# Gate and up products of experts 1 to 15 with the weights as the stationary operand, in halves of 64 array columns, and the turned token rows streamed

## The reference

```python
def ec_moe(x, router_w, w_gate, w_up, w_down):
    ...
    cap = n_tok * EC_CAPACITY // N_EXPERTS          # 64 sample tokens, 16 prompt tokens
    aff = jax.nn.softmax(jnp.einsum('btd,de->bte', x, router_w).astype(jnp.float32), axis=-1)
    gate, idx = lax.top_k(jnp.swapaxes(aff, 1, 2), cap)
    xe = x[bidx, idx]
    hid = jax.nn.silu(jnp.einsum('becd,edf->becf', xe, w_gate)) * jnp.einsum('becd,edf->becf', xe, w_up)
    ye = jnp.einsum('becf,efd->becd', hid, w_down) * gate[..., None].astype(x.dtype)
    return jnp.zeros_like(x).at[bidx, idx].add(ye)
```

## Time and profile before

| | |
|---|---|
| runs, us | 1419.07, 1413.60, 1416.11 (median 1416.11) |
| profiled execution: first to last instruction | 1413.9 us |
| PE busy | 1331.0 us (94%) |
| PE weight loads busy | 815.3 us (58%) |
| DVE, ACT, POOL busy | 697.4, 528.6, 280.4 us |
| mean granted TensorE clock | 0.982 of full |
| DMA | 333.82 MB, of which SP's queue 310.11 MB |

### The profile page before, as it was taken

The page is one execution under the profiler, slowest core; times in us unless marked ns, Lnnn a source line. Parts: engine busy times, 40 slices in busy tenths (PEclk is TensorE's granted clock), DMA queues, the critical chain, the costliest instruction groups (busy, mean ns, idle before and its releaser), DMA issues. The chain is left out here.

```text
span 1413.9 us, 27268 instructions
## 1 busy us (share of the span) xinstructions
PE 1331.0 (94%) x11153; PEld 815.3 (58%) x11153; DVE 697.4 (49%) x1634; ACT 528.6 (37%) x1221; POOL 280.4 (20%) x239
## 2 busy tenths in 40 slices
PE   5999998889899999999998999989899999999996
PEld 1755666766686444444448999555588444444443
DVE  1536614677635343334346646956654433334436
ACT  2723113666423222222226468665532322222213
POOL 0001103586002011111110030655301101111101
PEclk8999999999999999999998999999999999999997
DMA  9688961041526999999982012050043999999995
GB/s 364 237 328 304 350 217 27 23 158 34 194 107 257 369 377 375 374 378 373 387 307 74 1 64 68 1 223 1 1 183 125 374 368 378 378 377 381 376 350 180
DMA packets 105800, 333.82 MB, mean 236 GB/s; under 512 B 23182, under 2 KB 29164, under 8 KB 99532
## 3 DMA queue, kind: packets, MB, share of 16 engines
q1 hardware_dynamic: 99276, 310.11, 57.9%
q0 software_dynamic: 5824, 19.86, 5.9%
q10 hardware_dynamic: 576, 2.10, 0.4%
HBM read 308.13 MB, written 23.89 MB: 235 GB/s over the span
## 5 line engine op out<-in xcount | busy, mean ns | idle before, releaser
L1961 PE MATMUL psum<-wraw,proj 128*32 128x512 f32 x3072 | 399.6, 594 | 2.7 <-ACT proj L2071 1.2
L1967 PE MATMUL psum<-wraw,proj 128*16 128x256 f32 x3072 | 234.1, 379 | 0.6 <-ACT proj L2076 0.6
L1967 PEld LDWEIGHTS psum<-wraw,proj 128*16 128x16 f32 x3072 | 89.8, 97 | 229.5 <-issue 224.6
L1961 PEld LDWEIGHTS psum<-wraw,proj 128*32 128x32 f32 x3072 | 96.2, 110 | 74.1 <-issue 8.5
L1927 POOL DMA_INDIRECT x_rows<-modrow,idx x30 | 42.8, 1427 | 452.7 <-DVE modrow L2176 452.7
L2089 ACT ACTIVATE proj<-psum 128x320 f32<-128x320 f32 x32 | 14.0, 437 | 286.0 <-PE psum L2027 286.0
L2138 DVE TENSOR_SCALAR proj<-psum,proj 128x64 f32<-128x64 f32 x232 | 55.7, 313 | 106.5 <-PE psum L1949 106.5
L1336 POOL TENSOR_SCALAR ring<-ring,small 128x640 f32<-128x640 f32 x48 | 90.2, 1883 | 40.6 <-DVE small L1275 40.1
L2171 DVE SCALAR_TENSOR_TENSOR modrow<-psum,proj 64x512 f32<-64x512 f32 x60 | 44.9, 749 | 84.3 <-PE psum L1967 83.9
L2163 DVE TENSOR_TENSOR proj<-proj,psum 64x512 f32<-64x512 f32 x32 | 22.1, 690 | 128.1 <-ACT proj L2096 128.1
L1266 DVE TENSOR_REDUCE small<-psum 128x1 f32<-128x640 f32 (+1 forms) x80 | 57.3, 717 | 53.2 <-PE psum L1241 52.8
(11 more groups left out here) (520 smaller groups left out, 2437.6 us busy)
## 6 DMA issues: line engine op xcount, KB each, us to landing
wraw<-in_exp_w_gate_dram SPq DMA_DIRECT2D x128, 512.0 KB
wraw<-in_exp_w_up_dram SPq DMA_DIRECT2D x128, 512.0 KB
wraw<-in_exp_w_down_dram SPq DMA_DIRECT2D x128, 512.0 KB
ring<-in_ada_w_dram SPq DMA_DIRECT2D x29, 1024.0 KB, 6.5
hold<-in_ada_w_dram SPq DMA_DIRECT2D x14, 1024.0 KB, 6.6
ring<-in_ev_w_in_dram SPq DMA_DIRECT2D x4, 2048.0 KB, 12.3
xr<-x_rows SPq DMA_DIRECT2D x15, 512.0 KB, 7.4
proj<-in_ada_w_dram SPq DMA_DIRECT2D x5, 1024.0 KB, 9.0
```

The lines of the kernel that those rows point to most:

```text
L1961: mm = pe.matmul(psum[quad(q, 32), b, :], xs[:, quad(q % 2, 32)], pair[q // 2], start=first, stop=last)
L1967: mm = pe.matmul(psum[quad(q, CAPP), b, 0:QP], xs[:, CAPS:CAP], pair[q // 2][:, q % 2 * QP:(q % 2 + 1) * QP], start=first, stop=last)
```

## The change

The gate and up products of experts 1 to 15 swap their operands. The stationary operand is now 64 columns of weights; two such halves stand beside each other in the array's columns, and through each the 80 token columns of `xgT` (sample and prompt tokens together) are streamed. For each of the 8 blocks k, each of the two matrices and each of 4 blocks f of 128 hidden positions there are two matmuls of 64 x 80: 128 matmuls an expert where there were 64. The result has hidden positions in partitions and tokens in columns, in one bank for gate and one for up, which is what the down product needs: `turn_hidden` and `turned_hidden` are left only for expert 0. ACT has one silu of 128 x 320 and DVE one product of 128 x 320 straight into `hidT`, of which there are now two, for even and odd experts. Hidden position f x 128 + p now stands in partition p of block f, so the down matrices are loaded row by row in that order (`load_weights`, n == 2): each of the four DMAs reads one unbroken 512 KB, as 128 pieces of 4 KB as before. PSUM banks are dealt out anew: 5 and 3 for odd, 2 and 6 for even experts' hidden rows, 4 and 7 for down, and `tensor_last` goes to bank 0.

```diff
         def load_weights(sp, l, m, ready):
             n, e = EXPERT_ORDER[m]
-            src = A[EXPERT_W[n]][l, e].rearrange("(p k) n -> p (k n)", p=P)
...
+            if n == 2:
+                src = A[EXPERT_W[n]][l, e].rearrange("(f p) n -> f p n", p=P)
+                pieces = [src[i] for i in range(PARTS)]
+            else:
+                src = A[EXPERT_W[n]][l, e].rearrange("(p k) n -> p (k n)", p=P)
+                pieces = [src[:, i * w:(i + 1) * w] for i in range(PARTS)]
...
                 def into_hidden(e, h):
...
                         if e >= 2:
-                            pe.wait_ge(s["hid"], e)
+                            pe.wait_ge(s["hid"], e - 1)
...
                     for k in range(4 * h, 4 * h + 4):
-                        pair = [wraw[m % NSLOT][:, k * 512:(k + 1) * 512] for m in (gate_at, up_at)]
-                        samples(5, xgT[:, e % 2, k, :], pair, k == 0, k == KD - 1)
-                        mm = prompts(3, xgT[:, e % 2, k, :], pair, k == 0, k == KD - 1)
+                        rows = xgT[:, e % 2, k, :]
+                        for m, b in zip(both, hidden_banks(e)):
+                            for f in range(FB):
+                                for c in range(0, P, WT):
+                                    at = k * 512 + f * P + c
+                                    mm = pe.matmul(psum[c:c + WT, b, f * CAP:(f + 1) * CAP], wraw[m % NSLOT][:, at:at + WT], rows,
+                                                   start=(k == 0 and f == 0), stop=(k == KD - 1), skip_group_check=True)
...
                 for e in range(1, NE):
                     into_hidden(e, 0)
-                    turn_hidden(e - 1)
-                    if 1 < e < NE - 1:
+                    if e == 1:
+                        turn_first_hidden()
+                    elif e < NE - 1:
                         turn(e + 1)
...
                     down(e - 1)
-                turn_hidden(NE - 1)
                 if following:
                     following["tensor_last"](pe)
                 down(NE - 1)
...
                 def gate_hidden(e):                                   # ACT
                     act.wait_ge(s["mm"], PLACE_OF[1, e] + 1)
...
+                    act.activation(sgT, bank(hidden_banks(e)[0], FB * CAP), ACT.Silu).then_inc(s["hs"], 1)
...
                 def hidden(e):                                        # DVE
...
+                        dve.wait_ge(s["mm"], PLACE_OF[2, e - 2] + 1)
+                    dve.wait_ge(s["hs"], 3 + e)
+                    dve.tensor_tensor(hidT[e % 2], sgT.rearrange("p (f c) -> p f c", c=CAP), bank(hidden_banks(e)[1], FB * CAP).rearrange("p (f c) -> p f c", c=CAP),
+                                      ALU.mult).then_inc(s["hid"], 1)
```

86 lines of the change are left out of this document (46 added, 40 removed).

## The result

The kernel after takes 1424.10 us (median of 11 runs, 1419.23 to 1428.51), the kernel before 1416.29 us (11 runs on the same chip): ratio 1.0055, 95% interval 1.0039 to 1.0072. That is 7.8 us slower, where 1410 and a gain of 6 had been forecast. The profiled execution took 1424.36 us with a span of 1421.7 us.

What follows compares the result with a forecast made beforehand. The prediction took the weight DMAs (18.9 us an expert against PE's 17.1) as the bound; 1413.9 - 2.4 (layer 0) - 3.5 (layer 1) = 1408.0 us of span, plus 2.2 gave 1410 us, range 1400 to 1430.

Steps and rivals of the forecast that it cites:

- PE's new time: Experts on PE: gate and up products take 9.0 us, the period 15.5 us an expert, 1.6 less than before.
- Were PE alone the bound, 2 x 15 x 1.6 = 48 us would go: Both layers' expert stages: 48 us would be saved if only PE set the pace.
- Rival A: Gate and up products: PE cannot be fed, a pair costs over 0.19 us, total 1512 or 1560 us; chance 0.12.
- The pace of the weights: Expert weight loads: DMAs need 6.29 us a matrix, 18.9 us an expert, and keep that pace.
- What makes PE faster turns almost wholly into waiting for weights: Expert stages: PE catches the DMAs up near expert 9, then waits some 3 us an expert.
- the DMAs are slower than PE: Expert stages before the change: DMAs slower by 1.8 us an expert, living on ten slots filled ahead.
- Its start can move forward by about 0.3 us; I take 0.5: Start of expert 15: up 15 lands at 710.0, PE starts at 710.26, so only 0.5 us is gained.
- rival B: Instruction fetches: 0.48 MB more cost 29 us on one DMA engine, 2 us if spread; 1415 to 1439, chance 0.08.
- C: Clock rival: idling halves PE's clock; catching expert 15 in both layers loses up to 3.5 us each; 1412 to 1418, chance 0.10.
- I take 3.5: End of layer 1: terms sum to 3.6 us, rows read back only some 2.5 us earlier, so 3.5 us gained.
- the 1.35 us between the two down products: Between down 14 and down 15: with the turning of hidden rows gone, layer 1 saves all 1.35 us.
- 0.34 for faster: Chance of a time under 1409.0 us: 0.4 of the forecast's 0.60 plus rival D's 0.10.

Runs made afterwards that it cites:

- light traffic: Kernels before and after, loading only the first ten expert matrices of each layer, later products reading what stands in the slots: 1416.56 us (before) and 1369.05 us (after).
- split prompts: Kernel before with each 256-column prompt-row matmul of experts 1 to 15 split into two of 128: 1422.89 us, ratio 1.0045.
- only 15 in halves: Kernel before with the new products for expert 15 alone, in both layers, and the new layout of down throughout: 1419.88 us, ratio 1.0021.
- padded_before: Kernel before with 240 more wait instructions per expert on TensorE's queue in experts 1 to 15: 1731.55 us, ratio 1.2221.
- pool_padded: Kernel before with 240 more wait instructions per expert on GpSimd's queue in experts 1 to 13, both layers: 1581.55 us, ratio 1.1168.
- down_layout_alone: Kernel before with only the down matrices' new row order and hidden rows turned to match: 1413.93 us, ratio 0.9988.
- kept_busy: Kernel after with 12, 16 and 20 small matmuls ahead of the weight waits of experts 11, 12 and 14: 1424.17 us, ratio 1.0055.

## Why the prediction was wrong

**PE's new time: right.** 9.0 us forecast for the products, 9.07 to 9.2 undisturbed; 15.5 forecast for the period, 15.50 with the weights away. "Were PE alone the bound, 2 x 15 x 1.6 = 48 us would go": 47.5 with the weights away. Rival A is out (a pair at 0.14 us, not 0.19).

**The pace of the weights: nearly right, and it hid the error.** 18.9 us an expert became 19.2. "What makes PE faster turns almost wholly into waiting for weights" held. That "the DMAs are slower than PE" before the change was too strong: the kernel with light traffic takes the same time, PE and DMA were level.

**The step that failed first is "Its start can move forward by about 0.3 us; I take 0.5".** It assumed that up 15 still lands when it did in before. Counted from the first weight piece, up 14 lands 1.5 and 2.2 us later and up 15 2.6 and 2.0 (means of five profiles), and PE starts expert 15 2.9 us later in layer 0, not 0.5 earlier. That was rival B's mechanism: instruction fetches beside the weights. I gave B 0.08 and two prices, 29 us on one engine or 2 us spread. With split prompts the last pieces of up 14 and up 15 came 1.6 to 3.2 us late, between the two. Because PE waits for the last piece of one matrix near the end of each layer, even the small price lies on the path, twice. B's working had a slip: 27268 is the count of all engines' instructions, and by it 7440 more would be 0.40 MB. TensorE's own records are 22755, which gives the 0.48 MB that I wrote; measured are 0.46 (28 packets).

**B had a second half that I missed.** I priced the bytes and not the delay. A packet takes 1.06 us, but while the weights are issued the next starts 5.9 us later at the earliest, 6.4 in the median. An expert has some 660 instructions on TensorE's queue (512 for the products, 128 for down, 16 for turning, a few waits), 660 / 256 x 6.4 = 16.5 us, where its matmuls need 15.5. In mid-stage the mean period was 16.4 and 16.7 us, not 15.5 (single experts took 15.5 to 17.5), and the products of 15 took 10.0 us for 9.0. That the fetches set this pace, and do not merely follow it, rests on the run without weights, where both the "issue" gaps and the longer periods are gone.

**C was right in kind and misplaced.** The half clock caught expert 14, not 15, in both layers: 6.8 and 7.3 us for 4.6. Filling the waits cured it without moving the end: up 15 and the instructions were not there sooner. From the start of 14 to the end of down 15 after takes 39.1 us, where 35.4 are needed with light traffic (671.7 to 707.1) and before took 40.1. So PE kept 1.0 us of 4.7 and started 1.7 late.

**"I take 3.5" in layer 1** rested on the rows read back coming 2.5 us earlier. They follow the scatter-add of 14 by 8 us, and of the terms that I summed up to the end of down 15 the 1.35 us between the two down products did nothing for it. Even the kernel that gained 3.2 us in the experts of layer 1 gave 2.4 back behind them. In layer 0 DVE still waited 4.14 us for the token numbers (4.74 before), which were issued at 728.84 for 726.76: late with the products of 15.

**The range held the time, the chances did not.** That 1424.1 lies between 1400 and 1430 is luck as far as the mechanism goes: its upper part was there for C and for a B that costs up to 29 us on one engine. 0.34 for faster came from counting the costs of B and C as separate, unlikely mishaps. They came together here, with the late weights and instructions behind both.

What stays open: how much time the lower mean clock (0.972 for 0.982) costs, and so how the 7.8 us divide between late fetches and weights on one side and the clock on the other; why the kernel with only 15 in halves has it too (0.976 in 12 runs), and the 2 us by which timed runs of after exceed its profiles. How the fetches delay the last pieces, by one engine or several, the trace does not say.

## What to carry to other kernels

Count TensorE's instructions against the fetch rate, not only against its array time: at one packet of 256 per 6.4 us beside saturated weight loads, experts of 660 instructions took 16.4 to 16.7 us in the mean. And where the path waits for the last piece of a transfer, look at what additional fetch packets do to it: with 22 to 28 of them it came 1.5 to 3.2 us late here. Shortening the engine's work in a stage where the transfers are level with it first needs fewer bytes or instructions, and a look at which wait ends the stage: here an earlier scatter-add, not the last matmul. Of both kernels, a run with the transfers taken away tells which of the two bounds a stage (taking them away gained nothing for the kernel before, 55 us for the one after).

## What the runs showed of the hardware

- Instructions are fetched during the run, in packets of 16 KB for TensorE; 7200 instructions more are 28 packets more (`padded_before`), so a packet holds about 256. While weights are issued, with the DMA share at 1.04, the packets start 5.9 us apart or more (eight profiles with the new products, 67 to 69 gaps each), with light traffic down to 3.5. The Trainium skill (Trainium Architecture — The Big Picture, "The software stack") says that the instruction streams are brought into each engine's memory when the program is loaded. For a stream as long as this one that is not the whole of it: 117 packets are spread over this run.
- An instruction of two semaphore waits that are already met takes 106 ns of TensorE's queue (`padded_before`) and 87 ns of GpSimd's (`pool_padded`). Matmuls run beside it only until the queue is the bound.
- Four transposes of hidden rows take 0.71 us when each reads every fourth column (`before`) and 0.50 when it reads 128 columns side by side (`down_layout_alone`).
- With 80 columns streamed in f32 (both passes, loads included), two matmuls side by side in two halves of 64 array columns take 0.14 us together; one of 128 array columns takes 0.23 us.
- A keep-busy matmul of 128 columns in f32 is two records of 0.118 us: 0.236 us (40 records in 4.73 us, `kept_busy`).
